# Gate rows by DMA instead of by matrix product, and folded query-state, normaliser and sample rows, in a two-layer attention / mLSTM step

## What is computed

```python
b = jnp.cumsum(lf, axis=-1)
mt = b + jnp.maximum(m[..., None], lax.cummax(li - b, axis=2))
a = jnp.exp(b + m[..., None] - mt)
dmat = jnp.exp(jnp.where(causal, dlog, -jnp.inf))      # dlog from b, li and mt
qk = jnp.einsum('bhtd,bhsd->bhts', qs, k) * dmat
num = a[..., None] * jnp.einsum('bhtd,bhde->bhte', qs, S) + jnp.einsum('bhts,bhse->bhte', qk, v)
den = a * jnp.einsum('bhtd,bhd->bht', qs, n) + jnp.sum(qk, axis=-1)
hout = num / jnp.maximum(jnp.abs(den), jnp.exp(-mt))[..., None]
...
hn = hs * lax.rsqrt(jnp.mean(hs * hs, axis=-1, keepdims=True) + NORM_EPS) * g_head
```

## Time and profile before

| | |
|---|---|
| median of 3 runs | 2228.76 us (2226.25 to 2232.56) |
| the profiled execution | 2226.1 us, its span 2224.5 us |
| mean granted TensorE clock | 0.979 |
| TensorE busy | 2144.5 us, 96% |
| VectorE, ScalarE, GpSimd busy | 941.4, 676.8, 75.7 us |
| HBM read and written | 277.58 and 23.11 MB |

### The profile page before, as it was taken

The page is one execution under the profiler, slowest core; times in us unless marked ns, Lnnn a source line. Parts: engine busy times, 40 slices in busy tenths (PEclk is TensorE's granted clock), DMA queues, the critical chain, the costliest instruction groups (busy, mean ns, idle before and its releaser), DMA issues.

```text
span 2224.5 us, 37038 instructions
## 1 busy us (share of the span) xinstructions
PE 2144.5 (96%) x15828; PEld 1866.3 (84%) x15828; DVE 941.4 (42%) x1432; ACT 676.8 (30%) x1137; POOL 75.7 (3%) x126
## 2 busy tenths in 40 slices
PE   5899999999999999997899999999999999999998
PEld 2579989999999856667889999999899999996676
DVE  4344645546465422235433434334243525254224
ACT  4123434435344321225322222222222222223121
POOL 1000000000000100000000000000000000001000
PEclk8899999999999999998999999999999999999999
DMA  8883222232221588854434343453434244519622
GB/s 321 328 286 96 77 61 78 63 92 58 78 59 58 181 309 309 318 198 133 86 79 114 79 114 79 96 87 83 92 100 98 77 88 84 104 59 335 238 81 100
DMA packets 290527, 298.96 MB, mean 134 GB/s; under 512 B 8721, under 2 KB 213769, under 8 KB 288857
## 3 DMA queue, kind: packets, MB, share of 16 engines
q1 hardware_dynamic: 279504, 247.87, 39.7%
q0 software_dynamic: 10576, 48.45, 6.2%
q10 hardware_dynamic: 290, 0.32, 0.1%
HBM read 277.58 MB, written 23.11 MB: 135 GB/s over the span
## 4 chain that ended last, share of the span: by engine, by line
PE 86%; DMA 9%; DVE 2%; ACT 2%; issue 1%; DVEq 0%; ACTq 0%; SPq 0%
PE PJ L913 49%; PE PJ L1197 14%; DMA raw<-in_w_in_mlstm 5%; DMA obuf<-in_w_ada 3%; PE MX L1125 3%; PE PJ L939 3%; PE MX L1054 2%; PE MX L1063 1%; PE MX L1163 1%; PE MX L1077 1%; DMA arena<-in_x_prompt 1%; PE PJ L1219 1%; PE MX L1017 1%; PE MX L1411 1%; ACT w_hi L1472 1%
## 5 line engine op out<-in xcount | busy, mean ns | idle before, releaser
L913 PE MATMUL PJ<-h_hi,w_hi 128*128 128x272 f32 x3200 | 683.0, 295 | 2.4 <-DVE w_lo L1938 2.4
L913 PE MATMUL PJ<-h_hi,w_lo 128*128 128x272 f32 x3200 | 665.3, 290 | 0.0
L913 PE MATMUL PJ<-h_lo,w_hi 128*128 128x272 f32 x3200 | 663.4, 289 | 1.5 <-issue 1.5
L913 PEld LDWEIGHTS PJ<-h_hi,w_hi 128*128 128x128 f32 x3200 | 506.0, 190 | 26.4 <-issue 20.1
L913 PEld LDWEIGHTS PJ<-h_lo,w_hi 128*128 128x128 f32 x3200 | 506.4, 190 | 1.7 <-issue 1.7
L913 PEld LDWEIGHTS PJ<-h_hi,w_lo 128*128 128x128 f32 x3200 | 503.4, 190 | 0.0
L1938 DVE TENSOR_TENSOR w_lo<-raw,w_hi 128x2048 fp32r<-128x2048 f32 x94 | 215.4, 2292 | 305.5 <-ACT w_hi L1472 305.3
L1472 ACT ACTIVATE w_hi<-raw 128x2048 fp32r<-128x2048 f32 x94 | 179.4, 1909 | 57.4 <-DMA raw<-in_w_in_mlstm 42.3
L1197 PE MATMUL PJ<-w_hi,h_hi 128*128 128x512 f32 x448 | 181.5, 405 | 0.0
L1197 PE MATMUL PJ<-w_hi,h_lo 128*128 128x512 f32 x448 | 176.4, 394 | 0.0
L1197 PE MATMUL PJ<-w_lo,h_hi 128*128 128x512 f32 x448 | 176.1, 393 | 0.0
(11 more groups left out here) (396 smaller groups left out, 2231.2 us busy)
## 6 DMA issues: line engine op xcount, KB each, us to landing
arena<-in_w_ada SPq DMA_DIRECT2D x64, 1024.0 KB, 8.8
raw<-in_w_in_mlstm SPq DMA_DIRECT2D x52, 1024.0 KB, 17.1
raw<-in_w_in_attn SPq DMA_DIRECT2D x40, 1024.0 KB, 5.7
obuf<-in_w_ada SPq DMA_DIRECT2D x32, 1024.0 KB, 10.9
raw<-in_w_out_attn SPq DMA_DIRECT2D x16, 1024.0 KB, 12.9
raw<-in_w_out_mlstm SPq DMA_DIRECT2D x16, 1024.0 KB, 5.0
obuf<-in_w_in_mlstm SPq DMA_DIRECT2D x12, 1024.0 KB, 27.2
arena<-in_state_C POOLq DMA_DIRECT2D x8, 1024.0 KB, 15.8
```

The lines of the kernel that those rows point to most:

```text
L913: last = mm(PJ[:, 2 * pair + f, 0:HT], w, h[:, k, HT * f:HT * f + HT], start=(k == 0 and n == 0), stop=(k == KT - 1 and n == 2))
```

## The change

1. The three gate rows (`R[0]`, `R[1]`, `R[2]`, 8 heads x 544) are stored by GpSimd's queue into a scratch tensor in HBM, `row_spill`. For heads 1 to 7 the same queue loads the head's rows back, repeated over 128 partitions: three DMAs of 128 x 2 KB into `Dm`, `aB` and `emt`, one of 128 x 3 x 128 B into `sB`. They wait for `head_done` of the head before and stand behind that head's state load in the queue. Head 0 is as before (`opening(m)`). For the other heads the masking (`RBt`, `RS`), L1345, L1359 and ScalarE's copies into `aB` and `sB` go.
2. The denominators of p4 and p6 are added on VectorE first: `qn += Dm` (384 columns), `qn += Ds` (32 columns); TensorE then makes 128 + 384 columns in place of 512 + 384 in p4, and one product of 32 columns in place of two in p6.
3. p5 and p6: ScalarE scales the first half of the query-state result into `Dm[:, 0:256]`, VectorE adds the scaled second half (new semaphore `qs_done`), and p6 has one product with `C_SS` per value block in place of two; L1389 has 128 rows in place of 32.
4. p8: VectorE adds the two halves of `hsq` (544 columns, `hsum_done`), ahead of the state additions of p7; L1411 has two products in place of four.
5. Output stages: sample rows lie as 4 column quarters in the four partition groups. L1150 and L1171 become four products of 128 columns in four column tiles; `sample_square` and `sample_gated` run once per layer on 128 partitions; the small DMAs of `gs`, `xs` and `y_sample` move pieces of 512 B. The gate of the samples now goes to bank 2, so the first adaLN product of the next group waits for `mod_taken`.
6. Some semaphores are merged (`ct_steps`); the constants are 32 columns narrower.

```diff
+            for j in range(3):
+                pool.dma_start(row_spill[j], R[j]).then_inc(gl_in, 16)
+            pool.wait_ge(gl_in, 144)
+            def rows_of(it):
+                r, c = it
+                h = fixed(pool, r + c)
+                pool.wait_ge(gl_in, 144)
+                pool.wait_ge(head_done, val(1, 1, it))
+                for j, dst in enumerate((Dm, aB, emt[:, 0:TP])):
+                    pool.dma_start(dst, row_spill[j][ds(h, 1), 0:TP].broadcast_to([P, TP])).then_inc(row_in, 16)
+                pool.dma_start(sB, row_spill[:, ds(h, 1), TP:T].rearrange("j o t -> o j t").broadcast_to([P, 3, TS]))\
+                    .then_inc(row_in, 16)
...
             with pool.Fori(0, MH - 1) as r:
                 states((r, 0), True)
+                rows_of((r, 1))
...
 # TensorE: output stages
+                if j == 0 and is_gate(n - 1):
+                    pe.wait_ge(mod_taken, n - 7)
...
-                mm(MX[32 * g:32 * g + 32, 1, :], sel[0:MROWS + 1, X_GS:X_GS + TS], rows, start=True, stop=True)\
-                    .then_inc(mod_turned, 1)
+                for j in range(4):
+                    last = mm(MX[32 * j:32 * j + 32, 2, P * g:P * g + P], sel[0:MROWS + 1, X_GS:X_GS + TS],
+                              rows[:, P * j:P * j + P], start=True, stop=True)
...
-                mm(MX[32 * g:32 * g + 32, 1, :], sel[:, X_ST:X_ST + TS], scp[:, :], start=True, stop=True)\
-                    .then_inc(ysum_made, 1)
+                for j in range(4):
+                    last = mm(MX[32 * j:32 * j + 32, 1, P * g:P * g + P], sel[:, X_ST:X_ST + TS],
+                              scp[:, P * j:P * j + P], start=True, stop=True)
...
 # TensorE: memory, p1, p2, p4, p6, p8
-                    for j in range(3):
-                        last = mm(MX[:, 1 + j, :], fix[32 * j:32 * j + MH, C_ONE:C_ONE + P], RB[j],
+                    if opening(m):
+                        pe.wait_ge(rb_done, 2)
+                        for j in range(3):
+                            last = mm(MX[:, 1 + j, :], fix[32 * j:32 * j + MH, C_ONE:C_ONE + P], RB[j],
...
-                    mm(MX[:, 2, :], ones, Dm[:, :], start=True, stop=False)
-                    mm(MX[:, 2, P:TP], ones, qn[:, P:TP], start=False, stop=True).then_inc(num_ready, 1)
+                    mm(MX[:, 2, 0:P], ones, Dm[:, 0:P], start=True, stop=True)
+                    mm(MX[:, 2, P:TP], ones, qn[:, P:TP], start=True, stop=True).then_inc(num_ready, 1)
...
-                        mm(o, vs[0:TS, P * blk:P * blk + P], Ds[0:TS, :], start=True, stop=False)
-                        for c in range(2):
-                            mm(o, Dm[:, DV * c + P * blk:DV * c + P * blk + P], fix[:, C_SS + TS * c:C_SS + TS * c + TS],
-                               start=False, stop=(c == 1))
-                    mm(MX[:, 3, 64:64 + TS], ones[0:TS, :], Ds[0:TS, :], start=True, stop=False)
-                    mm(MX[:, 3, 64:64 + TS], ones, qn[:, TP:T], start=False, stop=True)\
-                        .then_inc(nums_ready, 1)
+                        mm(o, vs[:, P * blk:P * blk + P], Ds, start=True, stop=False)
+                        mm(o, Dm[:, P * blk:P * blk + P], fix[:, C_SS:C_SS + TS], start=False, stop=True)
+                    mm(MX[:, 3, 64:64 + TS], ones, qn[:, TP:T], start=True, stop=True).then_inc(nums_ready, 1)
...
-                        for blk in range(2):
-                            last = mm(MX[:, 1 + f, 0:HT], ones, hsq[:, blk, HT * f:HT * f + HT],
-                                      start=(blk == 0), stop=(blk == 1))
+                        last = mm(MX[:, 1 + f, 0:HT], ones, hsq[:, 0, HT * f:HT * f + HT], start=True, stop=True)
...
 # VectorE: memory
+                    dve.wait_ge(P_done, val(0, 1, m, 1))
+                    chain(tt(qn[:, P:TP], qn[:, P:TP], Dm[:, P:TP], ALU.add))
...
+                if p == 5:
+                    dve.wait_ge(qg_done, val(0, 1, m, 1))
+                    stt(Dm[:, 0:DV], MX[:, 2, DV:2 * DV], bm[:, NB + 1:NB + 2], Dm[:, 0:DV], ALU.mult, ALU.add)\
+                        .then_inc(qs_done, 1)
...
                 if p == 7:
+                    dve.wait_ge(hsq_done, val(0, 2, m, 2))
+                    tt(hsq[:, 0, :], hsq[:, 0, :], hsq[:, 1, :], ALU.add).then_inc(hsum_done, 1)
```

More of the change, by code:

```diff
@@ L108 @@
 C_OH, C_O3, C_SS = 305, 313, 337
-C_FIX = C_SS + 2 * TS
+C_FIX = C_SS + TS
 C_NEGD, C_NEGS = C_FIX, C_FIX + 768
@@ L203, in val, with opening @@
     return n if r is None else r * per + n
+def opening(it):
+    return it[0] is None and it[1] == 0
 def fixed(eng, value):
@@ L415, in trunk @@
                                                       sem("abs_done"), sem("abss_done"))
-        hout_done, hsq_done = sem("hout_done"), sem("hsq_done")
+        hout_done, hsq_done, hsum_done = sem("hout_done"), sem("hsq_done"), sem("hsum_done")
+        row_in = sem("row_in")
         h_free = sem("h_free")
-        hp_done, qc_ready, qg_done = sem("hp_done"), sem("qc_ready"), sem("qg_done")
+        hp_done, qc_ready, qg_done, qs_done = sem("hp_done"), sem("qc_ready"), sem("qg_done"), sem("qs_done")
         cu_ready, cnew_done, ss1_ready = sem("cu_ready"), sem("cnew_done"), sem("ss1_ready")
@@ L1170, in sample_sum @@
                 pe.wait_ge(mod_taken, g + (8, 20)[l] - 6)
-                mm(MX[32 * g:32 * g + 32, 1, :], sel[:, X_ST:X_ST + TS], scp[:, :], start=True, stop=True)\
-                    .then_inc(ysum_made, 1)
+                for j in range(4):
+                    last = mm(MX[32 * j:32 * j + 32, 1, P * g:P * g + P], sel[:, X_ST:X_ST + TS],
+                              scp[:, P * j:P * j + P], start=True, stop=True)
+                last.then_inc(ysum_made, 1)
             def square_sum(col):
@@ L1271, in _ @@
             pe.wait_ge(sc_s, 1)
-            for c in range(4):
-                last = tr(MX[:, 0, :].rearrange("p (g c t) -> p g c t", g=4, c=4)[:, :, c, :],
-                          ys[:, P * c:P * c + P], ident)
+            for g in range(4):
+                last = tr(MX[:, 0, P * g:P * g + P], ys[:, P * g:P * g + P], ident)
             last.then_inc(t_samp, 1)
@@ L1749, in _ @@
             out_root(0, 2, 1)
-            sample_square(0, 3)
+            sample_square(0)
             x_square(0)
@@ L2254, in out_product @@
                         i = n - (8, 20)[l]
-                        cols, rows = slice(512 * i, 512 * i + 512), slice(32 * i, 32 * i + 32)
+                        cols, part = slice(512 * i, 512 * i + 512), slice(P * i, P * i + P)
                         dve.wait_ge(gp_in, (96, 192)[l])
                         chain(tt(gp[:, cols], gp[:, cols], MX[:, 3, :], ALU.mult))
-                        tt(gs[rows, :], gs[rows, :], MX[rows, 1, :], ALU.mult).then_inc(mod_taken, 1)
+                        tt(gs[:, part], gs[:, part], MX[:, 2, part], ALU.mult).then_inc(mod_taken, 1)
                     else:
@@ L2418, in memory @@
                 h = c if r is None else r + c
-                if p == 0:
+                if p == 0 and opening(m):
                     ts(RBt[0:GP.stop, :], Rt[0:GP.stop, 0:TP], fix[0:GP.stop, ds(h + C_OH, 1)], None, ALU.mult).then_inc(rb_done, 1)
@@ L2583 @@
     args.append(nc.dram_tensor("x_spill", (P, KT * T), F32, kind="Internal").ap())
+    args.append(nc.dram_tensor("row_spill", (3, MH, T), F32, kind="Internal").ap())
     trunk(nc, *args)
```

145 lines of the change are left out of this document (79 added, 66 removed).

## The result

The changed kernel takes 2182.08 us (median of 4 runs, 2179.13 to 2183.31) against 2229.94 us of before (4 runs): a ratio of 0.978, 95% interval 0.9761 to 0.9798. On two other chips it took 2180.51 against 2224.16 and 2182.14 against 2225.60 (5 and 9 runs each time; ratios 0.9798 and 0.9794). So it gives 43.5 to 47.9 us.

The account below looks back on a forecast made before the run. TensorE, busy for 96% of the span, was taken as the bound, so stream time removed shortens the run. The terms sum to 38.4 us, less 1 for contention 37.4: 2228.8 - 37.4 = 2191 us, range 2183 to 2206.

Parts of the forecast that it names:

- p6: All 8 heads: three products of 32 columns fewer on TensorE, 0.89 us a head, 7.1 us.
- The upper bound (7.5 us): The most that p6 was allowed to give in the bounds of the sum, 7.5 of 43 us.
- the rival price for p6: Some 60 cycles of overhead a matmul, 0.025 us a record: p6 gives 1.2 us, the time is 2196.
- p1: Heads 1 to 7: three products of 512 columns on 8 rows, running together, go: 1.04 us a head, 7.3 us.
- p2: Heads 1 to 7: L1359, 96 columns, goes: 0.2 us a head, 1.4 us in all.
- p4: All 8 heads: 384 columns fewer on TensorE, the addition on VectorE: 0.64 us a head, 5.1 us.
- p8: All 8 heads: two of L1411's four products of 272 columns go: 0.91 us a head, 7.3 us.
- gate and sum: Output stages, L1150 and L1171, 8 times each: four 128-column tiles run together, 0.64 us each time, 5.1 us for each line.
- The covers: Slack before TensorE or VectorE would wait: 1.8 us at p8, 1.7 at p6, 23 to 36 for row DMAs.
- The charge of 1 us for contention: Whole run: 1 us lost because row DMAs delay weight loads in heads where loads are already late.
- Mild contention: Rival, chance 0.13: weight loads of `l1` late for TensorE, 2 us in each of 7 heads, 14 us, time 2205.
- The small products aren't worth their rows: Rival, chance 0.08: small products hide behind weight loads or 128-column tiles don't overlap; 27.5 us saved, time 2201.

Follow-up runs that it names:

- u_k32: Changed kernel with the two value products of p6 on 32 rows again in place of 128: 2180.54 us, a steady head 111.53 us.
- u_k32g: Changed kernel with those two value products on 32 rows again and reordered to stand side by side: 2187.07 us, a steady head 111.24 us.
- u_rows: Changed kernel without the row DMAs, gate rows by matrix product on TensorE in all heads: 2185.50 us, a steady head 112.51 us.
- x_more: Changed kernel with 1 MB more of DMA per head behind the row loads, the state copied to an unused tensor: 2179.38 us.
- x_shift: Changed kernel with eight more, long fulfilled waits in GpSimd's loop ahead of the row loads: 2176.45 us.

## Why the prediction missed

- **p6, the step that failed.** "Two of L1391 take 0.56 us ..., and one of L1389's kind 0.33 ... So 0.89 us": it measured 1.42, 8 x 0.53 = 4.2 us more. The rows give the time from start to start, and both the 0.56 and the 0.33 end at a change of form: 0.89 is three products and two changes (3 x 0.22 + 2 x 0.12). The other four changes stayed in the sum of what doesn't go, while zero-padding `vs` and `Ds` to 128 rows removes all of them. The upper bound (7.5 us) missed it in the same way. The Trainium skill says in "TensorEngine Tiling (Array Packing)", Key Properties, that changing the tiling mode drains TensorE; u_k32 and u_k32g agree that a change costs time, 0.12 to 0.13 us each, and no run here shows that it is a drain. The 60 cycles a matmul of the same page's Performance Considerations, the rival price for p6, fell: 0.22 to 0.235 us a product of two records, not 0.05. (The 2196 us that went with it left out the 1 us for contention; with it they are 2197.)
- **p1**: 1.26 us a head in place of 1.04, 7 x 0.22 = 1.5 us. "A step with the same column work as the scores alone" was L1381, which takes 1.36, while the scores alone take 1.14 (1681.45 to 1682.59). L1381 stands in column tiles, and two changes of form at 0.12 would be the difference; no run prices a change to column tiles by itself. The main reading, that three products of 8 rows run together, held: all three cost 1.26 us, and one product of that width 0.86.
- **p2** 0.23 for 0.2, **p4** 0.63 for 0.64, **p8** 0.92 for 0.91, **gate and sum** 0.62 and 0.61 for 0.64. Summed by measured steps: 9.9 in the output stages, 7 x 4.48 + 2.05 + 0.91 in `l1`, 44.2 us against 38.4.
- **The covers** held: 1.8 us ahead of p6, no wait of TensorE at p8, 40 us for the row DMAs.
- **The charge of 1 us for contention** isn't seen (u_rows, x_more). *Mild contention* as the rival had it, 2 us in each head, is out. *The small products aren't worth their rows* is out, 128-column tiles included.
- **"A microsecond taken out of TensorE's stream ... should be a microsecond of the end"** held for the whole (42.7 of 44.2) but not for each part: the output stages' 9.9 us, or the 7.3 us of p8, taken back alone, cost the time nothing that the runs can tell. Heads 3 and 4 gave 2.9 us less than their steps and the stretch ahead of `out0` lost 1.9, while the other heads of `l1` won 2.0 us at the clock and head 0 1.0 by its scatter. That these sizes nearly cancel is luck, not a rule.

Sized rightly, the same working gives 2228.8 - 44.2 = 2184.6 us. The remaining 2.5 us to the measured median are within the spread of either kernel's own runs, and before itself took 2224 to 2228 on the other chips.

## What to carry over

Price a TensorE step from the last backbone row ahead of it to the second behind it, and count changes of the array's form (here between 32 and 128 rows) as well as products: padding two 32-row products to 128 rows with zeros was worth 0.52 us, leaving two products out 0.47. Price an edit in its own stage, and then undo it alone and look at all stages: a gain can be real where it is made and be gone some stages later. Before reading a few microseconds of total as an edit's doing, profile both kernels several times and learn which stretches repeat (here to 0.01 us in steady heads without a fall of the clock, to 9 us in head 0).

## What the runs showed that was not expected

- A change of form between 128 and 32 rows costs 0.12 to 0.13 us, about half a true fp32 product of 32 columns (0.22 to 0.235 us).
- The granted clock can fall to half for 3.4 us in a stretch where TensorE never idles, right behind p6's small products; it cost 1.53 us in a steady head.
- A stop of 2.5 us cost about 1.7 more at a lower clock behind it (4.4 us at 0.61). A stop of 2.1 us at the same place in x_shift had the clock at 1.00 behind it.
- 1 MB more of DMA traffic a head behind the row loads doubled ScalarE's waits for weights (64.5 us for 29.3) and cost the time nothing measurable.
- 256 KB repeated over 128 partitions from one row in HBM landed 7.0 us after its issue and 48 KB in pieces of 128 B, issued behind it, 10.9 us after theirs.
